# Second block's heads on one Trainium2 core: weighted scores split before the next exponential, and one pooling chunk copied by VectorE

## The reference, cut to what matters

```python
s = jnp.einsum('bhctk,bhcsk->bhcts', q, k) * jnp.exp(dmat - m_t[..., None])
num = w_inter * einsum(q, c_in) + jnp.einsum('bhcts,bhcsv->bhctv', s, v)
den = w_inter * einsum(q, n_in) + jnp.sum(s, axis=-1)
h = num / jnp.maximum(jnp.abs(den), jnp.exp(-m_t))[..., None]
...
mix = jnp.concatenate([mlstm_out(h_lat, ...), pool_mixer(p[..., M_COLS:], ...)], axis=-1)
```

## Time and profile before

| what | us |
|---|---|
| median of 3 runs | 2939.49 (2939.06 to 2939.78) |
| time of the profiled execution | 2939.65 |
| its span | 2937.8 |
| TensorE busy | 2929.1 of 2937.8 |
| VectorE, ScalarE, GpSimd busy | 1795.9, 1130.7, 241.0 |
| TensorE busy from 2406 to 2510, the stage of heads | 101.84 of 104 |

### The profile page before, as it was taken

One profiled execution on the slowest core, in us unless ns is written; L12 is line 12 of the kernel. 1 busy time (PEld: TensorE's weight loads), 2 busy tenths in 40 slices (PEclk: granted clock), 3 DMA queues, 4 the chain that ended last, 5 costly groups with the idle time before them and its releaser, 6 DMA issues.

```text
span 2937.8 us, 36480 instructions
## 1 busy us (share of the span) xinstructions
PE 2929.1 (100%) x14809; PEld 2490.2 (85%) x14809; DVE 1795.9 (61%) x2671; ACT 1130.7 (38%) x1739; POOL 241.0 (8%) x202
## 2 busy tenths in 40 slices
PE   9999999999999999999999999999999999999999
PEld 8988888888888888888888899888889887888887
DVE  7867666865767876778857656332348668543234
ACT  4432333433534333324434345222235457432222
POOL 0300100000001200100000011000002006200001
PEclk9999999999999999999999999999999999999999
DMA  8454455344443433344434435222235341223222
GB/s 303 162 169 152 151 170 188 136 139 141 137 136 115 153 128 100 125 145 141 154 133 146 141 125 174 99 95 99 93 113 174 111 151 37 73 86 99 95 96 69
DMA packets 109623, 385.81 MB, mean 131 GB/s; under 512 B 12168, under 2 KB 15752, under 8 KB 109456
## 3 DMA queue, kind: packets, MB, share of 16 engines
q1 hardware_dynamic: 84816, 296.36, 30.0%
q10 hardware_dynamic: 24640, 87.12, 9.1%
HBM read 381.32 MB, written 2.11 MB: 131 GB/s over the span
## 4 chain that ended last, share of the span: by engine, by line
PE 98%; DVE 0%; ACT 0%; POOL 0%; issue 0%; DMA 0%; POOLq 0%; DVEq 0%
PE ps L527 30%; PE ps L529 30%; PE ps L528 30%; PE ps L742 1%; PE ps L757 1%; PE ps L743 1%; PE ps L621 1%; PE ps L656 1%; PE ps L593 0%; PE ps L594 0%; PE ps L597 0%; PE ps L630 0%; PE ps L1363 0%; PE ps L1362 0%; PE ps L1652 0%; PE ps L1639 0%
## 5 line engine op out<-in xcount | busy, mean ns | idle before, releaser
L2558 DVE TENSOR_TENSOR WL<-stage,WH 128x1024 fp32r<-128x1024 f32 x496 | 613.8, 1239 | 549.5 <-ACT WH L1694 548.8
L527 PE MATMUL ps<-HH,WH 128*128 128x512 f32 x2152 | 839.6, 390 | 0.1
L528 PE MATMUL ps<-HL,WH 128*128 128x512 f32 x2152 | 836.1, 389 | 0.0
L529 PE MATMUL ps<-HH,WL 128*128 128x512 f32 x2152 | 835.8, 388 | 0.0
L1694 ACT ACTIVATE WH<-stage 128x1024 fp32r<-128x1024 f32 x500 | 525.2, 1052 | 432.9 <-PE ps L529 425.1
L527 PE MATMUL ps<-GH,WH 128*128 128x512 f32 (+2 forms) x1687 | 577.7, 342 | 0.0
L528 PE MATMUL ps<-GL,WH 128*128 128x512 f32 (+2 forms) x1687 | 575.7, 341 | 0.0
L529 PE MATMUL ps<-GH,WL 128*128 128x512 f32 (+2 forms) x1687 | 575.7, 341 | 0.0
L529 PEld LDWEIGHTS ps<-HH,WL 128*128 128x128 f32 x2152 | 404.0, 188 | 84.3
L527 PEld LDWEIGHTS ps<-HH,WH 128*128 128x128 f32 x2152 | 404.3, 188 | 81.6 <-issue 1.1
L528 PEld LDWEIGHTS ps<-HL,WH 128*128 128x128 f32 x2152 | 404.3, 188 | 80.3
(11 more groups left out here) (326 smaller groups left out, 2934.7 us busy)
## 6 DMA issues: line engine op xcount, KB each, us to landing
stage<-ws SPq DMA_DIRECT2D x535, 512.0 KB, 3.4
MST<-wm ACTq DMA_DIRECT2D x154, 512.0 KB, 3.4
Z<-wm SPq DMA_DIRECT2D x10, 512.0 KB, 8.6
TAB<-consts ACTq DMA_DIRECT2D x7, 448.0 KB, 3.7
MST<-wm SPq DMA_DIRECT2D x6, 512.0 KB, 8.8
Z<-max_rows ACTq DMA_DIRECT2D x8, 256.0 KB, 4.6
out<-X SPq DMA_DIRECT2D x16, 128.0 KB, 1.8
X<-xT SPq DMA_DIRECT2D x2, 512.0 KB, 6.0
```

The lines of the kernel that those rows point to most:

```text
L527: e.matmul(o, wh, mh, start=start, stop=False, **more)
L528: e.matmul(o, wh, ml, start=False, stop=False, **more)
L529: return e.matmul(o, wl, mh, start=False, stop=stop, **more)
L2558: e.tensor_tensor(wl, src, wh.bitcast(F32), ALU.subtract).then_inc(wlo.sem, wlo.up(("w", i)))
```

## The change

1. A1, the first chunk of the pooling's group 1, is rounded by VectorE (`split_done`, `weights`), like B1, instead of by ScalarE. VectorE takes it, B1 and the low part of WQ in front of the first pooled mean.
2. ScalarE no longer waits for a free weight buffer before it writes the high part of WQ, which goes to `HELD`.
3. In head 0, ScalarE splits the tile 0/1/1 right after 0/1/0, ahead of the next chunk of weights and of the masked exponentials. VectorE makes the products of 0/2 and of 0/3 before the low part of that chunk of weights.
4. In heads 1 to 3, ScalarE writes the high part of h/0/0 before the exponential of h/1/0, and the high part of h/0/1 before the exponential of h/1/1.
5. At the end of head 0, ScalarE makes the exponential of 1/0/1 before the denominators of head 0.

```diff
         def split_done(i):
-            if chunks[i][0][0] == "poolm" and chunks[i][0][2] == 0:
+            if chunks[i][0][0] == "poolm" and chunks[i][0][2] == 0 and chunks[i][0][1] != 1:
                 return whi, "w", i
...
-                    if i >= NW:
+                    if i >= NW and wh is not HELD[0]:
                         act.wait_ge(*operands_free(i))
...
                 if h:
+                    weigh(h, 0, 0)
                     exponents(h, 1, 0)
-                    weigh(h, 0, 0)
+                    weigh(h, 0, 1)
                     exponents(h, 1, 1)
-                    weigh(h, 0, 1)
...
                 if h == 0:
+                    weigh(h, 1, 1)
                     weights(("po", 3), ahead=1)
                 masked_exponents(h, 2, 0)
                 masked_exponents(h, 2, 1)
-                weigh(h, 1, 1)
-                if h == 0:
+                if h:
+                    weigh(h, 1, 1)
+                else:
                     pool_out(2)
...
+                if h == 0:
+                    exponents(h + 1, 0, 1)
                 denominators(h)
-                if more:
+                if h and more:
                     exponents(h + 1, 0, 1)
...
-            weights(("pm", 1), ahead=0)
+            weights(("pm", 1), ahead=1)
             pool_mean(0)
-            weights(("pm", 1), ahead=1)
             pool_low(0)
...
                     masked(h, 3, 1)
-                    weights(("po", 3), ahead=1)
-                    pool_out(2)
                 weigh(h, 2, 0)
                 weigh(h, 2, 1)
...
+                else:
+                    pool_out(2)
                 weigh(h, 3, 0)
                 weigh(h, 3, 1)
                 if h == 0:
+                    weights(("po", 3), ahead=1)
                     pool_out(3)
```

## The result

The changed kernel takes 2943.28 us (median of 20 runs, 2941.14 to 2944.48), the kernel before 2939.11 (20 runs, 2937.93 to 2940.45): ratio 1.0014, 95% interval 1.0008 to 1.002. That is 4.2 us slower: less than the 0.2% named in the prediction, but more than nothing, since the interval ends above 1. The forecast was 2941.4 with a range up to 2943.0: the sign was right, the size was not.

A forecast was written before the change was run, and what follows sets the result against it. TensorE, busy 2929.1 of 2937.8 us, was taken as the bound. Terms -0.2 (head 0), +0.6, +1.1, +0.4 (heads 1 to 3) gave +1.9: 2941.55 profiled, 2941.4 as median, range 2937.6 to 2943.0.

The forecast's parts named there:

- the 0.2% named in the prediction: Whole kernel: the smallest difference a measurement can tell from no change, about 5.9 us.
- Part 1: Pooling chunk and WQ: TensorE's 0.56 wait at head 0's first product goes, plus 0.1 for the slow first matmul: -0.7 us.
- Part 2: Tile 0/1/1: TensorE's 1.26 wait for its low part goes, plus 0.1 and some 0.1 more: -1.5 us.
- Part 3: Rest of head 0, at tile 0/2/0: what comes back, leaving head 0 at -0.2 us, bounds -1.3 to +0.4.
- the terms -0.9 and +1.0: Tile 0/2/0: its high part at best 0.9 earlier; a second masked piece meeting GpSimd costs 1.0.
- the second meeting: Head 0: the moved weight chunk's low part on VectorE falls on GpSimd's low part of 0/2/0, up to +0.7.
- The first meeting: Head 0: a second masked piece on VectorE meets GpSimd's low part of 0/1/1, which follows 0/1/0 without pause, +1.0.
- The first step: Whole kernel: TensorE's time is its work plus waits; the change leaves the work untouched and only removes or adds waits.
- The prediction's own line on what would prove it wrong: Wrong if TensorE meets the last tiles without a wait, or if the stage ends earlier than now.
- Part 4: Heads 1 to 3: high parts moved ahead delay the exponentials and later tiles: +0.6, +1.1 and +0.4 us.
- the last rival: Heads 1 to 3: masked piece h/2/1 meets a whole GpSimd low part in each; 5.9 slower, 2945.4 us; chance 0.08.

The follow-up runs named there:

- e6: Kernel before with only A1 rounded by VectorE and WQ's high part written by ScalarE without waiting for a free buffer: 2938.72 us, ratio 0.9999.
- e2: Changed kernel with the high parts of h/0/0 and h/0/1 behind the exponentials again in heads 1 to 3: 2939.77 us, ratio 1.0003.
- e3: Changed kernel with idle matmuls filling both waits of head 0, 3 before scores 0/5 and 7 before tile 0/2/0: 2942.04 us, ratio 1.0011.
- e5: Changed kernel with VectorE's low parts of the weight chunk and the pool's output 2 ahead of the products of 0/2 again: 2942.22 us, ratio 1.0011.
- e10: e2 with 3 idle matmuls before scores 0/5 and 7 before tile 0/2/0 in head 0: 2939.62 us, ratio 1.0002.
- e11: Changed kernel with only the 7 idle matmuls before tile 0/2/0, the wait of 0.49 left empty: 2942.18 us, ratio 1.001.
- e4: Changed kernel with ScalarE's high part of 0/1/1 behind the weight chunk and masked exponentials again: 2941.01 us, ratio 1.0008.
- e8: e2 with head 0 reordered: masked piece 0/2/0 made in the pooling stage, its product and high part earlier: 2937.45 us, ratio 0.9995.
- e7: e6 with the exponential of 1/0/1 also made before the denominators of head 0: 2938.83 us, ratio 0.9998.
- e1: Kernel before with only the high parts of h/0/0 and h/0/1 ahead of the exponentials in heads 1 to 3: 2941.61 us, ratio 1.0009.

## Why the prediction was right and wrong

**Part 1 (-0.7): right.** The wait for WQ's low part is gone and the first product comes 0.68 earlier. e6 shows that alone it is worth only 0.2 to 0.3.

**Part 2 (-1.5): right, 0.25 too large.** Tile 0/1/1 comes without a wait, 1.93 early in all, of which 0.68 is part 1: 1.25. The wait was worth its 1.26 and not the 0.2 that I had added to it.

**Part 3 (-0.2): this step failed.** The bounds were -1.3 with no meeting of VectorE and GpSimd and +0.4 with both; I took -0.2, a value nearer to none. Both took place, and head 0 measured +0.40. VectorE and GpSimd after, in head 0 (masked pieces, the chunk's low part; then GpSimd's low parts of 0/1/0, 0/1/1, 0/2/0):

```profile
2422.06 1.40 DVE L3342 SCALAR_TENSOR_TENSOR SCR<-Z,GC,TAB 128x128 f32<-128x128 f32 x1
...
2423.38 1.38 DVE L3342 SCALAR_TENSOR_TENSOR SCR<-Z,GC,TAB 128x128 f32<-128x128 f32 x1
...
2424.68 0.34 DVE L3342 SCALAR_TENSOR_TENSOR SCR<-Z,GC,TAB 128x128 f32<-128x128 f32 x1
...
2427.46 1.21 DVE L2562 TENSOR_TENSOR WL<-stage,WH 128x1024 fp32r<-128x1024 f32 x1
...
2421.48 1.83 POOL L3690 TENSOR_TENSOR GL<-SCR,GH 128x512 fp32r<-128x512 f32 x1 [0.43 <-ACT GH L1714]
...
2423.26 1.35 POOL L3690 TENSOR_TENSOR GL<-SCR,GH 128x512 fp32r<-128x512 f32 x1
...
2427.94 1.86 POOL L3690 TENSOR_TENSOR GL<-SCR,GH 128x512 fp32r<-128x512 f32 x1 [3.33 <-ACT GH L1714]
```

GpSimd's low part of 0/1/1 now begins at 2423.26, right behind that of 0/1/0, and the second masked piece at 2423.38, so it ends at 2424.76 instead of some 2423.7. ScalarE's masked exponential hangs on it, and behind that, in ScalarE's order, six more steps and only then the high part of 0/2/0:

```profile
2427.25 0.62 ACT L1714 ACTIVATE GH<-SCR 128x512 fp32r<-128x512 f32 x1
```

It is later than the 2426.81 of the earlier trace rows, where I had it come earlier by up to 0.9. Then the chunk's low part holds GpSimd up by 0.56, 1.86 in place of 1.30. Tile 0/2/0 comes at +0.40, the upper bound; that it fits to the digit is luck, for the high part of 0/2/0 came 0.3 later, where the terms -0.9 and +1.0 give 0.1, and the second meeting cost 0.56 and not 0.7. The mistake was not in the mechanism or in its price but in the weighting: the low part of 0/1/1 comes without a pause because that is what edit 3 does. The first meeting is in each of the six traces that have this order (the change, e2, e3, e5, e10, e11): GpSimd begins 0.11 or 0.12 ahead of the second masked piece, which takes 1.37 or 1.38 every time. So it didn't come and go with tenths of a us, as I had argued. e4 (0/2/0 at -0.16) and e8 (-0.89) show it from the other side, e5 that the chunk's meeting is no loss of its own, since whatever stands at its place costs as much.

**The first step, "it can only remove or add waits": this failed too, by the half clock, +1.67.** The prediction put the work of TensorE at a fixed length, without a reason, and so the term for its clock at nothing. But behind the waits of 0.49 and 1.29 the clock falls for 3.4 us, in 12 of 20 runs by their mean clock, and the same matmuls take 0.43 in place of 0.23. It is this that carries the median over the end of the range, by 0.3: the runs at full clock have a median of 2942.02, within it. The prediction's own line on what would prove it wrong speaks only of waits. The Trainium skill, page "TensorE: Matmul & The Clock Gate", section "HAM oscillation — how this bites in real kernels", ties a fall to half clock to long waits for transfers that come back in every loop iteration. This case goes beyond it: no transfer is waited for here and nothing is repeated, and one wait of 1.29 behind one of 0.49, in a kernel that is busy for 99.6% of its span, was enough in part of the runs.'s wait of 1.26 standing alone was not, in any of the 93 runs of before beside the experiments, nor were those of 1.53 and 1.50 at the same tile in the 22 runs of e6 and e7.

**Part 4 (+0.6, +1.1, +0.4): right in the mechanism, and near in size.** From 2435.99 to 2457.41 the change loses 0.60, to 2478.89 another 0.99, to the end 0.74; together 2.33 against 2.1, and head 3 alone 0.3 more than forecast. Within a head, 0.8 goes at the sum of squares and 0.3 at the last tile of heads 1 and 2; in head 1 that 0.3 is no listed wait, though the forecast named one. The first tiles of heads 1 and 3 come 0.3 earlier. e1 has that gain at head 1 as well (+0.03 to -0.30), so it comes with edit 4, not with edit 5 alone, and the sum of squares takes it back. After, the sum of squares that TensorE waits for in head 1, then in head 2 VectorE's products of 2/1/0 and 2/1/1 and the masked piece 2/2/1, TensorE's sum of squares and last tile 2/5/1:

```profile
2448.80 1.05 PE L1380 MATMUL ps<-OC,SSQ 128*128 128x1 f32 x8 [0.55 <-ACT SSQ L2322]
...
2465.51 0.69 DVE L3351 TENSOR_TENSOR SCR<-ps,SCR 128x512 f32<-128x512 f32 x1 [0.45 <-ACT SCR L2285]
...
2466.64 0.69 DVE L3351 TENSOR_TENSOR SCR<-ps,SCR 128x512 f32<-128x512 f32 x1 [0.45 <-ACT SCR L2285]
...
2467.85 1.31 DVE L3342 SCALAR_TENSOR_TENSOR SCR<-Z,GC,TAB 128x128 f32<-128x128 f32 x1
...
2471.28 1.05 PE L1380 MATMUL ps<-OC,SSQ 128*128 128x1 f32 x8 [0.57 <-ACT SSQ L2322]
...
2482.69 0.50 PE L527 MATMUL ps<-GH 128*128 128x512 f32 x1 [0.18 <-POOL GL L3690]
```

The start of the head has moved by 2.8 (2457.41 to 2460.22), so the product of 2/1/0 is 0.4 late (0.57 forecast) and that of 2/1/1, at 2462.86 before, 1.0 late (1.1 forecast). What I had called the last rival, with 0.08, did happen in part: the masked piece h/2/1 meets a low part of GpSimd in each head, 1.31 here. The rule of the Trainium skill that the prediction weighed, page "SBUF — State Buffer", section "SBUF: two separate sides", has the later of the two wait for the whole of the earlier. The trace agrees: 0.34 alone, 1.31 behind a low part that began 0.13 earlier. But it had met one before as well, for 0.87, which the price of that rival overlooked. So only 0.4 was added, and VectorE mostly made that good with a sum of two directions of 0.69 (at 2469.87) instead of 1.00. Before, in head 2:

```profile
2464.06 0.87 DVE L3338 SCALAR_TENSOR_TENSOR SCR<-Z,GC,TAB 128x128 f32<-128x128 f32 x1
...
2465.64 1.00 DVE L3368 TENSOR_TENSOR SCR<-SCR 128x512 f32<-128x512 f32 x1
```

**The sum.** By the shifts: 0.40 in head 0, 2.33 in the heads, 1.67 for the clock: 4.40, and 4.17 by the medians. Forecast: -0.2 and 2.1. That is 2.5 more than the forecast's 1.9: 0.6 is part 3, 1.7 the clock, in the twelve runs that set the median, and 0.2 part 4. The miss is only 1.9 (2943.28 to 2941.4) because 0.6 goes the other way: the kernel before stood at 2939.11 and not at 2939.49, which is 0.4 and has nothing to do with the change, and the medians differ by 0.2 less than the traces.

Not settled: why the clock falls in twelve runs of twenty and not in all. Only one run of each kernel has a trace, so what the waits looked like in the eight at full clock is not known, and a kernel that moves the waits by some tenths on purpose was not run. Nor was one that fills the wait of 0.49 and leaves that of 1.29, so that it takes both is argued, from the single waits of 1.26 to 1.53 that left the clock up; e5's two runs at 0.999 show that one longer wait, of 1.72, may do it as well.

## What to carry to other kernels

When one engine writes strictly in order, a step that is moved ahead to remove a wait brings its successor on the next engine with it: look at what stands beside that successor, and count a meeting of VectorE and GpSimd as sure where the order brings it about; here it came in six traces of six. To begin a high part "as soon as it can" ahead of an exponential only helps if its input is there; where it isn't, the engine stands idle and everything behind comes late: here the second product by 1.0 us, and TensorE by 0.6 to 1.0 a head. A piece that is cheap alone and dear beside GpSimd (0.34 or 1.4) belongs in a stage where GpSimd is idle: e8 moved one, and with it the products and high parts behind it, and ends 1.4 us ahead of e10 (-1.04 against +0.39), which has the same heads and kept the full clock as well. And waits of 0.5 and 1.3 us close together may cost another 1.2 to 1.7 in clock.

## What the runs showed of the hardware

- The granted clock of TensorE fell to 0.50 (1.2 GHz) for 3.4 us after waits of 0.49 and 1.29 in the traces of the change and of e2. The mean clock of a run was 0.999 instead of 1.0 in 12 of 20 runs of the change, in 5 of 11 of e2 and in 2 of 11 of e5, with one wait of 1.72; in none of 33 with the later wait filled by seven idle matmuls (e3, e10, e11), and in none of 93 of the kernel before, whose longest wait there is 1.26. The stretch costs 1.67 where it stands, and some 1.2 by the end.
- VectorE's masked piece takes 0.34 alone. Where GpSimd began a low part about 0.1 earlier, it ends 0.1 to 0.2 after that low part: it takes 1.30 to 1.38 beside one of 1.3, 0.55 beside one of 0.51 and 1.10 beside one of 1.06 (the last two in head 0 after). And GpSimd's low part takes 1.86 instead of 1.30 when it begins 0.48 behind a row of 1.21 on VectorE.
- The point at which TensorE's matmuls go from 0.43 to 0.22 apart at the start of the kernel lies at another moment in each trace, which shifts everything behind it by up to 1.6 us from trace to trace. Two spans of this kernel that differ by 1.5 us say nothing; single matmuls in head 0, with that drift taken off, agree within 0.1 between kernels with the same orders.
